# Second expert projection of the last 128 tokens by fetched rows instead of dense matmuls

## The reference, cut to what matters

```
def peer_ffn(h, w_query, sub_keys, u_tab, v_tab):
    ...                                   # two top-16 searches a head, then the best 16 of their 256 sums
    expert_idx = jnp.take_along_axis(cand_i, pos, axis=-1)     # cand_i = first key * 128 + second key
    gates = jax.nn.softmax(best_s, axis=-1)
    def one_block(args):                  # a block of 128 tokens
        h_blk, i_blk, g_blk = args
        u_sel = u_tab[i_blk]                                   # 128 tokens x 128 picks x 1024
        act = jax.nn.gelu(jnp.einsum('td,thkd->thk', h_blk, u_sel))
        w = (g_blk * act).astype(h.dtype)
        return jnp.einsum('thk,thkd->td', w, v_tab[i_blk])     # the second expert projection
```

## Time and profile before

| what | value |
|---|---|
| median of three runs | 3238.48 us |
| profiled execution: span | 3240.0 us |
| PE busy | 3171.5 us (98%) |
| DVE busy | 2060.2 us (64%) |
| ACT busy | 1248.9 us (39%) |
| POOL busy | 425.9 us (13%) |
| mean DMA rate | 141 GB/s |
| chain that ended last | PE 91%, DVE 6%, ACT 1% |
| mean granted TensorE clock | 0.993 |

### The profile page before, as it was taken

The page is one execution under the profiler, slowest core; times in us unless marked ns, Lnnn a source line. Parts: engine busy times, 40 slices in busy tenths (PEclk is TensorE's granted clock), DMA queues, the critical chain, the costliest instruction groups (busy, mean ns, idle before and its releaser), DMA issues.

```text
span 3240.0 us, 37547 instructions
## 1 busy us (share of the span) xinstructions
PE 3171.5 (98%) x14084; PEld 2513.9 (78%) x14084; DVE 2060.2 (64%) x3455; ACT 1248.9 (39%) x2295; POOL 425.9 (13%) x186
## 2 busy tenths in 40 slices
PE   8999999999999999999999999999999999999999
PEld 7877778878778656767778888888888888888887
DVE  7678354367898899546646896777761455555554
ACT  4365222233223322235433335999982211111111
POOL 0000000014132000000002444333334000000000
PEclk9999999999999999999999999999999999999999
DMA  5243324332242454221122444676867555555553
GB/s 211 59 126 124 102 71 146 121 109 95 72 155 84 143 172 134 72 79 52 59 91 95 133 139 137 176 206 193 219 177 231 205 187 190 188 189 190 187 190 115
DMA packets 285845, 455.77 MB, mean 141 GB/s; under 512 B 148952, under 2 KB 156248, under 8 KB 285280
## 3 DMA queue, kind: packets, MB, share of 16 engines
q1 hardware_dynamic: 150560, 409.84, 37.9%
q10 hardware_dynamic: 135104, 43.52, 6.0%
HBM read 372.01 MB, written 81.26 MB: 140 GB/s over the span
## 4 chain that ended last, share of the span: by engine, by line
PE 91%; DVE 6%; ACT 1%; issue 1%; DMA 0%; POOL 0%; ACTq 0%; DVEq 0%
PE psum L644 91%; DVE wl L1489 1%; ACT wh L1077 1%; DVE yb L1701 0%; DVE psum L1865 0%; DVE trig L1584 0%; DVE lb L1692 0%; DVE st L1942 0%; DVE cs L1699 0%; DVE y L1703 0%; DVE trig L1587 0%; DVE trig L1586 0%; DVE trig L1589 0%; DVE trigw L1588 0%; DVE trigw L1585 0%
## 5 line engine op out<-in xcount | busy, mean ns | idle before, releaser
L644 PE MATMUL psum<-h_hi,wh 128*128 128x512 f32 x2144 | 857.0, 400 | 32.7 <-DVE h_lo L1633 13.2
L1489 DVE TENSOR_TENSOR wl<-ring,wh 128x1024 fp32r<-128x1024 f32 (+2 forms) x322 | 375.7, 1171 | 747.4 <-ACT wh L1077 746.4
L644 PE MATMUL psum<-h_lo,wh 128*128 128x512 f32 x2144 | 849.2, 396 | 0.0
L644 PE MATMUL psum<-h_hi,wl 128*128 128x512 f32 x2144 | 849.2, 396 | 0.0
L1077 ACT ACTIVATE wh<-ring 128x1024 fp32r<-128x1024 f32 (+2 forms) x492 | 504.6, 1027 | 813.5 <-PE psum L644 789.3
L2235 POOL TENSOR_TENSOR wl<-ring,wh 128x1024 fp32r<-128x1024 f32 x170 | 423.0, 2489 | 1784.3 <-ACT wh L1077 1784.3
L644 PEld LDWEIGHTS psum<-h_hi,wh 128*128 128x128 f32 x2144 | 406.4, 190 | 133.1 <-issue 40.6
L644 PEld LDWEIGHTS psum<-h_hi,wl 128*128 128x128 f32 x2144 | 405.8, 189 | 95.8
L644 PEld LDWEIGHTS psum<-h_lo,wh 128*128 128x128 f32 x2144 | 406.3, 190 | 88.5 <-issue 1.7
L644 PE MATMUL psum<-ews_hi,wh 128*128 128x512 f32 x1024 | 404.1, 395 | 0.7 <-ACT ga L1456 0.7
L644 PE MATMUL psum<-ews_hi,wl 128*128 128x512 f32 x1024 | 404.0, 395 | 0.0
(11 more groups left out here) (384 smaller groups left out, 3776.6 us busy)
## 6 DMA issues: line engine op xcount, KB each, us to landing
ring<-tables SPq DMA_DIRECT2D x256, 512.0 KB, 3.6
acts_scratch<-ga SPq DMA_DIRECT2D x128, 256.0 KB, 2.2
gates_scratch<-stage ACTq DMA_DIRECT2D x8, 4096.0 KB, 26.2
abuf<-acts_scratch SPq DMA_DIRECT2D x128, 256.0 KB, 3.8
gbuf<-gates_scratch SPq DMA_DIRECT2D x128, 256.0 KB, 4.0
ring<-w_up SPq DMA_DIRECT2D x44, 512.0 KB, 3.6
ring<-w_modb SPq DMA_DIRECT2D x32, 512.0 KB, 3.6
ring<-w_moda SPq DMA_DIRECT2D x16, 512.0 KB, 5.6
```

The lines of the kernel that those rows point to most:

```text
L644: return nc.tensor.matmul(out, lhsT, rhs, start=first, stop=last, **kw)
L1489: TT(wl, slot(t, 0, size[t]), wh.bitcast(F32), ALU.subtract).then_inc(S("low_by_ve"), 1)
```

## The change

For the last 128 tokens (`TD` = 384 onward) the second projection is no longer dense. In the dense part every matmul, product and buffer has 384 columns. The gates of the last block are kept in SBUF (`gate_s`); only the first three blocks are turned and spread (96 groups of four tokens, six stores). From the keys of the last block DVE works out, in integers and floats, where each pick's row lies in the weight tiles: two pieces of 512 floats (2 KB), in two different tiles (`piece_of`), and where its activation lies in `acts_scratch` (`act_of`). POOL then issues indirect DMAs, each for one pick of all 128 tokens (one token a partition): two for the pieces of the row and one for the activation. DVE multiplies activation and gate and adds the scaled row to one of two sums of 128 x 1024. PE turns the sum by eight transposes into the last 128 columns of the eight banks. The cast of the product moves from DVE to ACT. The rest of the diff merges semaphores under new names with the same meaning.

```
-                    last = three(psum[:, 4 * half + c, :], whl(e, 4 * kk + c), ews, b % NV, b == 0, b == PK - 1)
...
+                    last = three(psum[:, 4 * half + c, 0:TD], whl(e, 4 * kk + c), ews, b % NV, b == 0, b == PK - 1)
+                    if m == PK // 2 - 1 and kk == 1:
+                        if half == 0 and c == 0:
+                            pe.wait_ge(S("rows_summed"), PK + 1)
+                        dc = 4 * half + c
+                        last = nc.tensor.transpose(psum[:, dc, TD:T], accs[:, 0, dc * P:(dc + 1) * P], ident[:, :])
...
# POOL, behind the low halves of the first projection
+            def pick_row(k):
+                if k >= NV_ROWS and k % 2 == 0:
+                    gp.wait_ge(S("rows_summed"), k - NV_ROWS + 2)
+                for half in range(2):
+                    g.indirect_dma_start(out=vrow[k % NV_ROWS][:, 512 * half:512 * (half + 1)], out_offset=None, in_=pieces,
+                                         in_offset=bass.IndirectOffsetOnAxis(ap=piece_of[half][:, k:k + 1], axis=0))\
+                        .then_inc(S(f"rows_loaded{k // 2 % (NV_ROWS // 2)}"), 16)
+            def pick_acts(n):
+                for k in range(n * PICK_GROUP, (n + 1) * PICK_GROUP):
+                    g.indirect_dma_start(out=act_s[:, k:k + 1], out_offset=None,
+                                         in_=acts_d.rearrange("j p t -> (j p t)").unsqueeze(1),
+                                         in_offset=bass.IndirectOffsetOnAxis(ap=act_of[:, k:k + 1], axis=0))\
+                        .then_inc(S(f"acts_picked{n % 2}"), 16)
+            ...                       # waits: picks, gates_staged, gates_parked
+            for k in range(NV_ROWS):  # NV_ROWS = 10
+                pick_row(k)
+            for k in range(4):
+                gp.wait_ge(S(f"act_parked{k}"), 16 * (PK // 4))
+            for n in range(2):
+                pick_acts(n)          # PICK_GROUP = 16
+            for k in range(NV_ROWS, PK):
+                if k % PICK_GROUP == 0 and k // PICK_GROUP + 1 < PK // PICK_GROUP:
+                    pick_acts(k // PICK_GROUP + 1)
+                pick_row(k)
...
# DVE
-                v.tensor_copy(ews[0][:, b % NV, :], er[:, b % 2, :]).then_inc(S("ew_hi"), 1)
+            def add_row(k):
+                if k % PICK_GROUP == 0:
+                    ...               # wait for the group's activations, share_of = act_s * gate_s
+                ve.wait_ge(S(f"rows_loaded{k // 2 % (NV_ROWS // 2)}"), 64 * (k // NV_ROWS + 1))
+                acc, by = accs[:, k % 2, :], share_of[:, k:k + 1]
+                ...                   # k < 2: multiply only
+                    ins = STT(acc, vrow[k % NV_ROWS], by, acc, ALU.mult, ALU.add)
+            gated(0)
             for b in range(4):
-                gated(b)
+                gated(b + 1)
+                rest_of_gated(b)
...
             for k in range(PK):
-                if k + 4 < PK:
-                    gated(k + 4)
+                if k + 5 < PK:
+                    gated(k + 5)
                 if k + 3 < PK:
                     rest_half(k + 3)
+                if k + 4 < PK:
+                    rest_of_gated(k + 4)
+                while added < PK and (added + 1) * (PK - LAG - 2) <= (k + 1 - LAG) * PK:   # LAG = 8
+                    add_row(added)
+                    added += 1
# ACT
+                if v + 4 < PK:
+                    high_of_gated(v + 4)      # the cast of the product, 128 x 384
                 high_after(TILE[f"vo{v}"])
# DVE, once, behind the picks of the last block: 13 operations of 128 x 128 that fill act_of and piece_of
```

More of the change, by code:

```diff
@@ L44 @@
 TG = 64
+TD = T - P
+NV_ROWS = 10
+ONCE = {"vecs": 16, "bsrow": 32, "x": 48, "cum": 64, "keys": 96}
+PICK_GROUP = 16
+LAG = 8
 SW = 2 * T + 2 * P
@@ L71 @@
 PICKS_AT = (21, 29, 36, 44)
-SPREAD_OF = [[n for n in range(T // 4) if n // SPREADS == j - SPREAD_AT] for j in range(PK)]
+SPREAD_OF = [[n for n in range(TD // 4) if n // SPREADS == j - SPREAD_AT] for j in range(PK)]
 STAGES = []
@@ L164 @@
     projection(f"k{_u}")
-stage("f", ["BT"], False, lambda k: ("f_read", 1))
+stage("f", ["BT"], False, lambda k: ("f_step", 1))
 for _u in range(2):
@@ L301, in build @@
         acts_d = nc.dram_tensor("acts_scratch", (PK, P, T), F32, kind="Internal").ap()
+        pieces = io["tables"].rearrange("n p (k c) -> (n p k) c", c=512)
         def V(name):
@@ L411, in build @@
         one_col = sm(2 * HEADS - 1)
+        token = sm(1)
         epsc, silu_c = V("eps"), sm(KD)
@@ L1472, in _, with high_of_gated @@
                     park_gates(n)
+            def high_of_gated(b):
+                act.wait_ge(S("ew_raw"), b + 1)
+                if b >= NV:
+                    tile_used(act, TILE[f"vo{(b - NV) // 2 * 2 + 1}"])
+                A(ews[0][:, b % NV, :], er[:, b % 2, :], ACT.Copy).then_inc(S("ew_hi"), 1)
+            for b in range(4):
+                high_of_gated(b)
             for v in range(PK):
+                if v + 4 < PK:
+                    high_of_gated(v + 4)
                 high_after(TILE[f"vo{v}"])
@@ L2159, in _ @@
             assert spread_block(0) % 2 == 1
-            for n in range(T // 4):
+            for n in range(TD // 4):
                 if n % (P // 4) == 0:
@@ L2169, in _ @@
                     stage_gates(n - 2)
-            for n in (T // 4 - 2, T // 4 - 1):
+            for n in (TD // 4 - 2, TD // 4 - 1):
                 stage_gates(n)
@@ L2244, in _ @@
                 low(f"ui{j}")
+            def pick_row(k):
[11 more added lines that the diff above has]
+                        .then_inc(S(f"acts_picked{n % 2}"), 16)
+            gp.wait_ge(S("picks_ready"), NB + 1)
+            gp.wait_ge(S("gates_staged"), TD // 4)
+            for k in range(2):
+                gp.wait_ge(S(f"gates_parked{k}"), 16 * (TD // TG // 2))
+            for k in range(NV_ROWS):
[8 more added lines that the diff above has]
+                pick_row(k)
 HEAD_SCALE = float(P) ** -0.5
```

132 lines of the change are left out of this document (85 added, 47 removed).

## The result

The changed kernel takes 3184.09 us (median of four, 3183.15 to 3198.79) where the kernel before, on the same chip, takes 3240.14 (3238.48 to 3244.09): ratio 0.9835, 95% interval 0.9814 to 0.9856. It is 56 us faster; 183 were forecast. The profiled execution has a span of 3182.0 us.

What follows compares the result with a forecast made beforehand. PE, busy 98%, was taken as the bound. 3240.0 less 171.4 (second projection) and 15.2 (spreading), plus 5 for DMA delays, gave 3058.4 us of span, 3057 us as median; range for 8 in 10: 3046 to 3190.

Steps and rivals of the forecast that it cites:

- Matmuls of 384 columns, 0.1757 us, 4.22 us per tile: Second projection on PE: each matmul falls from 0.2325 to 0.1757 us, a tile from 5.58 to 4.22 us.
- spreading 15.2 us: First projection with spreading: 32 of 128 groups go, each 0.475 us of PE, saving 15.2 us.
- end of the stage: End of second projection: PE waits about 2 us for the sum of the rows, then eight transposes take 0.9 us.
- The positions of the pieces: Before the first one-hot rows: 13 DVE operations, about 3.5 us, covered by 10 us before ACT wants those rows.
- DVE per tile: Second projection: DVE needs 3.66 us per tile, 3.8 with gaps, of 4.22; row addition 1.22 us.
- DMA engines, 4.1 us per tile and 5 us of losses: Second projection: 1.486 MB per tile takes 4.1 us of 4.22, plus 5 us for delayed rows; rival, engines pace it, 0.14.
- The cast, taken as gone from DVE and hidden on ACT: Second projection: the cast leaves DVE; ACT is then busy 1.5 of 4.22 us per tile.
- POOL's price c = 1.1 us, just under the 1.31 at which rows would be late: Second projection: POOL time per indirect DMA, 384 of them; rows are in time for c up to 1.31 us.
- 322 c + 127: Length in us of the second projection if POOL's price c exceeds 1.31 us and rows pace it.
- POOL paces the rows: Rival, second projection: c between 1.31 and 1.87 us, giving 3119 us at 1.5 and 3183 at 1.7; chance 0.19.
- The rival of mutual hold-up, c = 2.1: Second projection: POOL and DVE delay each other, stage 806 us, total 3315 us, slower than before; chance 0.17.

Runs made afterwards that it cites:

- the two runs in which POOL's pace is the only delay or nearly so: Changed kernel with the first four casts moved into the first projection, 3112.18 us; changed kernel with activations gathered one by one between the rows, 3098.75 us.
- the burst of words: Changed kernel with rows by plain SP DMAs, activation product left out, and 32 unread word gathers on POOL without a pause: median 3090.42 us, ratio 0.9537.
- the first three runs of the experiments: Changed kernel without activation gathers, without row gathers after the first ten rows, and without either: 3073.23, 3109.55 and 3074.83 us.

## Why the prediction was wrong, and where it was right

*Matmuls of 384 columns, 0.1757 us, 4.22 us per tile; spreading 15.2 us; end of the stage.* Right: 0.1754 us, 4.22 us, 15.1 us, and 2 us at the end. The positions of the pieces cost nothing: PE's chain starts at 2010.21 for 2010.39.

*DVE per tile.* Right in size: 551 and 552 ns for product and remainder (0.554, 0.559), 1.28 for the row (1.22 taken), within its bounds. Where nothing is late DVE is busy 82% of the time, where 3.8 of 4.22 us was expected.

*DMA engines, 4.1 us per tile and 5 us of losses.* Right in size: share 1.00 at 350 GB/s in the run without POOL, and no loss.

*The cast, taken as gone from DVE and hidden on ACT.* Wrong. Its duration is hidden (0.52 us of 4.22), its place is not: the first four stand behind the last gelu of ACT, 7.4 us. The step priced the instruction and not the queue in front of it.

*POOL's price c = 1.1 us, just under the 1.31 at which rows would be late.* Mis-sized, and decisive: 1.25 undisturbed, 1.50 to 1.52 with DVE beside it. By the prediction's own formula, 322 c + 127, that gives 3119 to 3126 us; the two runs in which POOL's pace is the only delay or nearly so stand at 3112.18 and 3098.75. The formula is thus 7 us too high for the groups of 16 at 1.50 (its stage of 610 us is one of 599.7), and it was not made for activations one by one. Why it is high no run tests; it lets every late row delay PE in full, though DVE writes low halves three tiles ahead. So the rival "POOL paces the rows" was the case, for 43 to 56 us above the 3055.88 of the mended kernel. With the right c the forecast would still have been some 60 us below 3184.09: this step alone does not explain the miss. That 3184 lies inside the stated range is luck, because the range's upper end stood for c = 1.7 and not for what happened. The row nearest to the operation, SP's plain issue of 0.38 us, was no guide; what held was that a gather costs the same for 4 bytes, 512, 2 KB or 4 KB a piece, so that cutting rows in two pieces doubled the price.

*The rival of mutual hold-up, c = 2.1.* Half right, and a quarter of the size. POOL's gathers stretch from 0.95 to 1.36, 1.98 and, rarely, 2.97 us beside DVE, 0.25 on average; in the changed kernel the 118 gathers that meet no DVE instruction take 0.946 us, the other 266 take 1.295. DVE loses nothing on average: its row addition takes 1.28 us with and without gathers beside it. The Trainium skill, "SBUF — State Buffer", section "Who interferes with whom", infers that additions on DVE would not stop the writing of descriptors. The stretched gathers differ from that, in one direction only; a gather also reads its addresses from SBUF, and no run takes the two apart.

*What no step had: PE held up while POOL issues without a pause.* 34.4 us at tiles 2 and 3, most of 13.8 at 22 to 24 and part of what follows. The prediction let PE wait for operands alone. On one chip the runs show what brings it on (unbroken gathers, of 4 or 512 bytes), its size (24 us for 32 of them at the opening) and its cure (pauses). They also show that unbroken gathers are not enough: the run with early casts issues 384 without a break and has none of it, and one kernel is timed at 3055 and at 3074. The same page of the Trainium skill says that PE and ACT never wait on anyone for SBUF; in these runs PE waits, for whatever it is. What it waits for stays open. It is not the DMA engines (share 0.12 in the burst of words), not operands (the gaps stand where PE's program has no wait), and not the clock (0.70 us between starts, where the lower level gives 0.32). A late fetch of instructions does not show either: the DMA queue that the profile marks "instruction" brings PE's next 16 KB at 2525.8 us in 0.93 us and again at 2582.0, some five tiles further, as in runs without a hold-up. The count of finished tiles reaches ACT late as well in some runs: the last gelu starts 4.4 us after PE's last matmul of the first projection in the changed kernel, and 7.5 us after it in the first three runs of the experiments. It is 0.04 us in the run without POOL, but also in the runs with activations one by one and with rows in one piece, whose gathers are in the air by then. That hints at the path of semaphores, and proves nothing. Whether the recording of the profile has a part in it these runs can't say either.

The 128 us between 3184.09 and 3055.88 are thus, roughly: 11.8 of the opening's gap (7.4 for the order on ACT and 4.4 for the late count), 34.4 of the first hold-up, and some 82 of late rows and further hold-ups, which the runs do not part. They feed each other: a hold-up stops POOL's next gathers, which wait for rows to be added, and a POOL at its limit cannot make it up. The mended kernel is 185.6 us faster than before (3241.49 on its chip), near the 183 that were forecast, but with four edits that the change did not have (early casts, activations one by one, rows in one piece, the first words spaced). Its stretch and its page:

```profile
2600.00:3000.00 400.00, 400.00 (x2274) 400.00 (x2273) 328.66 (x395) 139.99 (x190) 261.64 (x201) 1.00 0.98 353
```

```profile
PE 2984.7 (98%) x13961; PEld 2462.8 (81%) x13961; DVE 2051.5 (67%) x3408; ACT 1227.4 (40%) x2166; POOL 755.9 (25%) x443
```

POOL is busy 262 of 400 us there instead of 299, and PE is back at 98%.

## What to carry to other kernels

Price indirect DMAs by their number, not by their bytes: some 1.25 us of GpSimd for each gather of 128 pieces, 1.5 beside a busy VectorE, in this kernel; where they pace a stage, merge pieces first. An instruction moved to another engine is paid in that engine's program order: look at what stands before it at the start of the stage, not only at the steady state. Spread GpSimd's DMAs over the tiles that need them instead of issuing them in bursts, and time more than one execution of a kernel that has bursts.

## What was unexpected of the hardware

- An indirect DMA of 128 words of 4 bytes holds POOL as long as one of 128 pieces of 512 bytes, 2 KB or 4 KB (0.94 to 0.96 us, and 0.30 between two).
- Beside two-input DVE instructions it takes up to 2.97 us in the changed kernel, 1.295 on average; DVE's row additions stay at 1.28 us.
- PE's matmuls can fall to starts 0.70 us apart, or a multiple of it, while such DMAs are issued without a pause, with the DMA engines nearly idle: on one chip some 24 us for 32 of them, in all eight executions, nothing when every second is followed by a pause of 1.3 us. On another chip four runs with unbroken gathers show none of it.
- DMA engines moved 353 GB/s over 400 us, at a share of 0.98, without delaying a tile.
